# Moving the next short tile's scores and ScalarE's three passes ahead of the short tile's transpose and copy (stick-breaking attention, first block)

## What is computed

```
z    = (q @ k.T) * SB_SCALE                 # strict: key position < query position
sp   = where(strict, softplus(z), 0)
excl = cumsum(sp, reverse=True) - sp        # sum over the later keys
a    = where(strict, exp(log_sigmoid(z) - excl), 0)
out  = a @ v
```

## Time and profile before

| what | value |
|---|---|
| median of 3 runs | 3790.58 us |
| lowest and highest run | 3786.0 and 3791.27 us |
| span of the profiled execution | 3784.3 us (the page has no other time of this execution) |
| PE busy | 3616.2 us, 96% of the span |
| ACT busy, DVE busy | 1216.1 us (32%), 1805.3 us (48%) |
| first `turn` to last `probs` copy of the attention stage | 77.4 us to 383.1 us of the span |

### The profile page before, as it was taken

How to read it: one execution, slowest core, us unless ns; L and a number is a source line. 1 busy time by engine, 2 the same in 40 slices (tenths; PEclk the granted TensorE clock), 3 DMA queues, 4 the chain that set the end, 5 groups by cost and what they waited for, 6 DMA issues and landing times. The chain is left out here.

```text
span 3784.3 us, 48486 instructions
## 1 busy us (share of the span) xinstructions
PE 3616.2 (96%) x17484; PEld 2956.1 (78%) x17484; DVE 1805.3 (48%) x3405; ACT 1216.1 (32%) x2273; POOL 1341.8 (35%) x800
## 2 busy tenths in 40 slices
PE   7997898999999999999999999998999999999997
PEld 6776677888888888788888888886888686868686
DVE  4666544244444445566666666666303424242412
ACT  4777243200000003455545555556101202020200
POOL 3211201233333222565565566563333131313331
PEclk9997899999999999999999999998999999999998
DMA  3100101111111113432222422211413020202231
GB/s 95 29 12 6 42 31 73 56 62 46 49 50 50 46 34 79 56 52 51 53 51 48 37 40 36 37 37 56 150 51 100 28 73 23 78 23 73 95 133 67
DMA packets 201142, 208.81 MB, mean 55 GB/s; under 512 B 12479, under 2 KB 155886, under 8 KB 200958
## 3 DMA queue, kind: packets, MB, share of 16 engines
q1 hardware_dynamic: 181390, 155.23, 17.5%
q10 hardware_dynamic: 19568, 50.93, 3.7%
HBM read 174.61 MB, written 31.52 MB: 54 GB/s over the span
## 5 line engine op out<-in xcount | busy, mean ns | idle before, releaser
L877 PE MATMUL ps<-all_u_hi,kept_w_hi 128*128 128x512 f32 x1952 | 784.7, 402 | 1.8 <-PEq L486 1.8
L881 PE MATMUL ps<-all_u_hi,kept_w_lo 128*128 128x512 f32 x1952 | 763.1, 391 | 0.0
L880 PE MATMUL ps<-all_u_lo,kept_w_hi 128*128 128x512 f32 x1952 | 761.3, 390 | 0.0
L827 POOL CAST kept_w_hi<-kept_w_raw 128x1024 fp32r<-128x1024 f32 x116 | 127.2, 1096 | 1210.1 <-PE ps L877 710.5
L1554 POOL TENSOR_SCALAR even_probs<-even_probs,even_stat 128x640 f32<-128x640 f32 (+1 forms) x250 | 428.0, 1717 | 347.8 <-DVE even_stat L1995 347.8
L881 PEld LDWEIGHTS ps<-all_u_hi,kept_w_lo 128*128 128x128 f32 x1952 | 366.7, 188 | 79.2
L877 PEld LDWEIGHTS ps<-all_u_hi,kept_w_hi 128*128 128x128 f32 x1952 | 368.5, 189 | 67.9 <-POOL sb_w_lo L829 2.0
L880 PEld LDWEIGHTS ps<-all_u_lo,kept_w_hi 128*128 128x128 f32 x1952 | 368.1, 189 | 66.2
L1811 ACT ACTIVATE even_probs<-even_probs,even_stat 128x128 f32<-128x128 f32 (+7 forms) x256 | 199.1, 778 | 300.8 <-DVE even_stat L1989 300.8
L829 POOL TENSOR_TENSOR kept_w_lo<-kept_w_raw,kept_w_hi 128x1024 fp32r<-128x1024 f32 x116 | 285.3, 2459 | 9.3
L877 PE MATMUL ps<-kept_w_hi,all_u_hi 128*128 128x512 f32 x640 | 250.5, 391 | 7.6 <-DVEq L2874 7.2
(11 more groups left out here) (417 smaller groups left out, 7267.5 us busy)
## 6 DMA issues: line engine op xcount, KB each, us to landing
kept_w_raw<-in_even_w_in_dram SPq DMA_DIRECT2D x64, 512.0 KB, 7.4
kept_w_raw<-in_odd_w_in_dram SPq DMA_DIRECT2D x48, 512.0 KB, 3.8
kept_w_raw<-in_w_up_dram SPq DMA_DIRECT2D x16, 512.0 KB, 4.0
mlp_w_raw<-in_w_up_dram SPq DMA_DIRECT2D x16, 512.0 KB, 4.0
kept_w_raw<-in_w_down_dram SPq DMA_DIRECT2D x16, 512.0 KB, 3.5
mlp_w_raw<-in_w_down_dram SPq DMA_DIRECT2D x16, 512.0 KB, 3.5
scratch_h<-residual SPq DMA_DIRECT2D x8, 1024.0 KB, 4.6
residual<-scratch_negc ACTq DMA_DIRECT2D x16, 512.0 KB, 5.5
```

The lines of the kernel that those rows point to most:

```text
L827: nc.gpsimd.tensor_copy(hi, raw).then_inc(w_hi.sem, 1)
L877: ins = nc.tensor.matmul(dst, lh, rh, start=first, stop=False)
L880: nc.tensor.matmul(dst, lh, rl, start=False, stop=False)
L881: return nc.tensor.matmul(dst, ll, rh, start=False, stop=last)
```

## The change

Two moves, both at k = 2 (the short tile's step). On PE the scores of the next short tile stand in front of `turn(h)` instead of behind it. On ACT the three passes over these scores stand in front of `probs_out(h)` instead of behind it. Nothing is added or removed, and DVE, POOL and SP have the same programs.

```diff
@@ tensor @@
                     nxt = following(h)
+                    if k == 2 and exists(c + 1):
+                        scores(SHORT, c + 1)
                     turn(h)
                     if k == 0 and exists(c + 2):
                         scores(LONG, c + 2)
-                    if k == 2 and exists(c + 1):
-                        scores(SHORT, c + 1)
                     if h and k != 1:
                         weigh(h - 1)
@@ scalar @@
+                    if k == 2 and exists(c + 1):
+                        soft(SHORT, c + 1)
                     probs_out(h)
                     if k == 0:
...
                         probs(SHORT, c)
-                    elif exists(c + 1):
-                        soft(SHORT, c + 1)
```

## The result

| | before | the change |
|---|---|---|
| median of 20 runs each | 3788.61 us | 3793.7 us |
| lowest and highest | 3783.87 and 3792.22 us | 3791.16 and 3798.61 us |
| ratio, 95% interval | | 1.0015 (1.0008 to 1.0021) |
| profiled execution, time and span | span 3784.3 us | 3793.61 us, span 3791.8 us |

The change is slower by 0.15%, 3 to 8 us by the interval. That is clear of zero, and 0.15% is inside the 0.2% that the prediction called no difference.

What follows compares the result with a forecast made beforehand. PE was taken to lead the rounds with projections, PE-ACT hand-offs and a low clock to shape the last. Terms -0.6 + 2.2 = +1.6 us on 3790.6 gave about 3792 us, range 3785 to 3799.

Steps and rivals of the forecast that it cites:

- What bounds it: Whole stage: PE leads in rounds with projections; in the last, PE and ACT hand work over; DVE, POOL, SP cost nothing.
- Filled waits given back at the long turn: Rounds with projections: PE's filled waits are mostly lost again waiting for ACT's later copy out of T; sum -0.6 us.
- the +0.1 of the prediction: One-block short tiles, rounds with projections: the long turn comes at 197.1 instead of 196.99, whole gain given back, +0.1 us each.
- the last section: Profile signs: ACT's copy waits down a third or more, rounds within 0.5 us of 78.8, last round 1 to 4 us longer.
- The last round: Round without projections: the late copy delays long turns and the long Abs behind them; sum +2.2 us, ends -1.5 and +7.7.
- the three-block tiles: Last round, two steps: the copy frees T near 332.95, so the long turn starts 0.45 us later each, +0.9 together.
- The four-block tiles: Last round, two steps: long turn 1.1 us late, partly regained by long scores at 2.4 GHz; +0.8 each, +1.6 together.
- is filled by the three passes: ACT's gap before the short copy, 0.70, 0.64 or 2.46 us in three traced cases, is taken up by the moved passes.
- The rule against the change: Skill's advice to rotate matmul groups through banks: T does not rotate, so by it alone all 31 steps would pay.
- Rival 1: T held too long in all rounds: 7 to 12 us with projections, 3 to 8 last, about +15, 3806 us; chance 0.08.
- Rival 2: PE's filled waits are kept: 6.6 us in rounds with projections, 1.5 in the last; -8.1 us, 3782.5; chance 0.08.
- Rival 3: Last round: shorter waits bring PE's clock back toward 2.4 GHz; -5 to -15 us, about 3781; chance 0.06.

Runs made afterwards that it cites:

- the best version: Kernel before with short scores at k = 1 behind the turn, ACT's old order, second transpose bank in the last round: 3776.97 us against 3788.81, ratio 0.9967.
- early scores, ACT's move and two banks: The change with short scores one half-step earlier on PE, at k = 1, and a second transpose bank in the last round: 3780.43 us, ratio 0.9980 to before.

## Why the prediction was right, and where its terms were off

**What bounds it: right.** What moved lies between PE and ACT, within the stage. No run changed DVE's or POOL's program, so that they play no part is read from the waits alone: ACT waits for neither of them more than before, and PE waits for DVE in the rounds with projections only at L1120, 4.4 us before and 6.0 in the change.

**Filled waits given back at the long turn: right, for two reasons instead of one.** In the rounds with projections the sum was to be -0.6 us; the trace has +0.6 from the first copy of round 1 to that of the last, and the kernel with the change in these rounds alone -0.03% (-0.12 to +0.06%). The one-block tile of the earlier trace rows in the changed kernel:

```profile
193.26 0.33 PE L1151 MATMUL ps<-all_ident,sb_probs_short 128*128 128x128 f32 x1 [0.25 <-ACT sb_probs_short L1245]
...
194.31 0.60 ACT L1234 ACTIVATE sb_soft_short<-ps 128x512 f32<-128x512 f32 x1
...
196.14 0.26 ACT L1254 ACTIVATE sb_probsT<-ps 128x128 f32<-128x128 f32 x1
...
196.54 0.63 PE L1151 MATMUL ps<-all_ident,sb_probs_long 128*128 128x128 f32 x4 [0.67 <-ACT sb_probsT L1254]
```

PE's wait fell from 0.84 to 0.25 and 0.67 appears at the long turn: from the short turn to the long one it is 3.28 us, before 3.05. This is the +0.1 of the prediction with 0.23 measured. Half a round later, at 206.13 us, the four-block tile's long turn waits 0.22 for the copy where I had 0.3. By width, from the first copy of a cycle to that of the next in rounds 2 and 3: one block costs 0.11 to 0.35 us (+0.1 forecast), two blocks nothing (0), three blocks -0.28 in the first half of a round and +0.12 in the second (-0.3), four blocks 0.01 to 0.11 and once 0.53 (+0.1). So rounds 2 and 3 were to be 0.2 us shorter each and came out 0.6 and 0.8 longer, past the 0.5 us around 78.8 that the last section allowed.

**The last round: the right mechanism, one term half its size.** The prediction had +2.2 us, the trace +3.6. Read from copy to copy, the three-block tiles cost 0.48 and 0.24 (I had 0.45 each). The four-block tiles cost 1.80 and 1.66, where I had 0.8 each. Of that, the turn was 1.30 us late (326.51 less 324.03, less the 1.18 from before), near the 1.1 of the prediction. From the turn to the long Abs it was then 2.97 us, before 2.48: 0.5 lost where 0.3 was to be won. The step that failed is the sentence that the long scores "then fall into a stretch at 2.4 GHz". The score matmul at 328.25 us still takes 0.63 us, the time of 1.2 GHz, and so does the next, at 328.68. The trace before had shown full clock from 325.75 us on:

```profile
325.75 0.42 PE L1138 MATMUL ps<-sb_k_hi_hi,sb_q_hi_lo 128*128 128x512 f32 x1
```

I carried that moment over into a kernel in which PE stood idle for 1.09 us just ahead of it; whether this idle time is what held the clock down is not shown. The two-block tile gave 0.9 back once and nothing the second time, the one-block tile nothing; 0 and -0.3 were forecast.

**A wait that was missed.** The last section forecast that ACT's 21.5 us before its copies would fall by a third or more. It fell by 15.3, and all of it came back before the short Abs. I had worked this wait out once, for the four-block tile, and not seen that it takes the place of the old one nearly everywhere. So the sentence that ACT's gap before the short copy "is filled by the three passes" is wrong: scores moved by one place on PE are still behind what PE has queued, a weigh and projections.

**The size: partly luck.** The difference was forecast at +1.6 us and is 5.1. The forecast of 3792 us comes within 2 us of the measured 3793.7 only because it starts from the median of three runs, 3790.6, and 20 runs have 3788.6.

**The rule against the change.** Perfetto Trace Analysis, section "Optimizing Tensor Performance", of the Trainium skill asks for groups that rotate through banks. The runs agree: with T alternating between two banks the same order takes 64.3 us and not 71.6 for the last round. By the rule alone all 31 moves would have paid. In round 2 the long turn waited 0.22 to 0.67 us for the copy at three of the eight short tiles, came 0.31 us behind it at one, and 1.1 to 2.2 us behind it at four. With the change in the first three rounds alone the time can't be told from the kernel before.

**Rivals.** Rival 1 (T held everywhere, +15 us) did not come in the change. ACT's move alone has its total, 3803.75 us for 3806, but not its split: 4.6 us in the rounds with projections and 11.3 in the last, where the rival had 7 to 12 and 3 to 8. Rival 2 (the waits kept) is what PE's move alone does in the rounds with projections, -4.2 us of the -6.6 at most (78.8 + 78.6 + 78.8 against 76.7 + 77.9 + 77.4). Rival 3 (the clock comes back) went the other way: the last round's clock fell to 0.62, below the 0.65 to 0.73 named.

## What to carry to other kernels

Before work is moved ahead of a copy that empties a buffer, look at who refills that buffer and what stands behind the refill in its queue: here the copy was short, and all that waited for it was not. When a wait of an in-order engine is to be filled, move the producer of the filling work at least as far ahead as its consumer, and check in the new profile that the wait did not reappear at another instruction, by adding up the engine's waits before and after, and its busy time where the clock moves. A move that loses with one buffer can win with two, so try both before the order is given up.

## What the runs showed of the hardware

Four transposes took 1.06 us at 1.2 GHz and 0.61 at 2.4, so an order of work that keeps the clock down pays in the matmuls themselves. From the first to the last copy of the last round the same instructions kept PE busy for 45.7 us in the best version, at a granted clock of 0.75, 49.5 before (0.70), 54.0 in the change (0.62) and 59.8 with ACT's move alone (0.52).

The clock did not follow the sum of PE's idle time in that round. That was 16.2, 18.6, 17.6 and 19.5 us in these four, and least, 14.0 us, with early scores, ACT's move and two banks, at a clock of 0.70. The kernels here do not show what it followed. Nor do they show how much of the 3.6 us of the change is waits and how much clock: no run held one fixed while the other moved.
